# Weight splitting by whole chunks: one ScalarE and one VectorE instruction for two units

## The chip, the cores and the metric

The kernel runs on one core of a Trainium2 chip. The metric is the device time of one execution in microseconds, the median of several runs; lower is better. An execution is also profiled once, and all times of single instructions come from that execution. In this text TensorE is also called PE, ScalarE ACT, VectorE DVE, and GpSimd POOL, as in the rows of the profile.

## The reference

Two layers of a decoder trunk over 256 tokens of width 2048, all in float32. Per layer:

```
h      = rms_norm(x)
proj   = h @ w_in[l]                  # q, k, v, indexer q/k/weights, GLU input, memory q, 3 gates
y_attn = sparse_attention(...) @ w_attn_o[l]      # 64 keys of 256, chosen by an indexer
y_mem  = cross_attention(mq, memory keys/values) @ w_mem_o[l]
y_conv = conformer_conv(glu_in) @ w_conv_o[l] + conv_o_b[l]     # depthwise, 31 taps
x      = x + (g0 * y_attn + g1 * y_mem + g2 * y_conv) @ w_out[l]
x      = x + square(relu(rms_norm(x) @ w_up[l])) @ w_down[l]    # 2048 -> 8192 -> 2048
```

## The kernel before

**Split matmuls.** Each float32 product is made of three reduced-precision ones. A weight `raw` is split into `hi` (raw rounded to the matmul's fp32r type, by ScalarE) and `lo` (raw minus hi, by VectorE); activations have been split in the same way. A product is then a_hi x hi + a_hi x lo + a_lo x hi.

**Chunks and units.** Weights stream from HBM in chunks of 1 MB, 2048 columns per partition. `raw` holds four chunks. A chunk is two units of 1024 columns; `hi` and `lo` hold four units each, that is two chunks. The whole program is 1008 units, used in order. In nearly all of them the unit is 12 matmuls of 512 columns (in the up projection 16 matmuls). In the group G_IKW the weight is only 80 columns wide, so its units are short: 160 columns to split and six small matmuls. Groups G_IQ0 and G_IKW alternate chunk by chunk, steps 16 to 31 of a layer.

**Steps.** Every engine's program is written out as one list of steps, one per unit. In step n ScalarE and VectorE first call `split` for unit n and then do whatever else is planned for that step (`side(n, l)`, `merge`, `mlp`, `x_side`); TensorE does unit n and then the transposes and small matmuls that are planned after it. Within an engine the order is fixed; between engines there are only semaphores. Four of them carry the weights:

- `landed[c]`: the chunk has come from HBM; ScalarE waits for it in the even unit.
- `unit_done`: starts at 4 and goes up by one when TensorE has finished a unit. ScalarE waits in `split` until `unit_done` is n+1, which is to say until unit n-4 is done and its place in `hi` and `lo` is free.
- `hi_ready`: ScalarE to VectorE, one per unit.
- `lo_ready`: VectorE to TensorE, one per unit; the loader on the sync queue waits for two of them before it overwrites a chunk of `raw`.

**What else hangs on the steps.** TensorE waits for results that ScalarE or VectorE produce in a later-numbered step than the unit that it is at. The places that matter here:

- Transposes go through two PSUM banks (`tp`, helper `fill`). A fill waits until the bank's last tile but one has been taken. Most tiles are taken four steps after their fill (`EMPTY_AFTER`).
- `norm_fill` after units 10, 18 and 26 of the output projection (`X_BLOCK_DONE` 12, 20, 28) waits for `scaled`, which VectorE gives in steps 12, 20 and 28, after `add_block` and `scale_block`. The last quarter of the first layer's MLP has the same three places 32 steps later.
- In the output projection unit 6 waits for the second `merged` tile, which VectorE takes in step 8, and the first `merged` fill, after unit 3, waits for `attention_merge` in step 4.
- In each merge block of 32 units, unit 26 needs the accumulator that VectorE empties in step 27 (`GATE_TAKEN`), unit 28 the one it empties in step 29.
- In the first MLP quarter the norm fills after unit 1 wait for `scale_block` in step 2, and unit 3 waits for their taking in step 4. In every quarter unit 4g waits for the accumulator that VectorE frees in step 4g+1.
- The eight index score pairs come after units 49 to 52 and 54 to 57 (`INDEX_PAIR_AT`); a pair waits until ScalarE's relu of the pair before it has emptied the bank, four steps later than that pair's unit.
- The twelve attention heads (`HEAD_AT`, units 77 to 115) send tiles `p` and `o` through the same two banks, mixed with `q`, `conv_out` and `conv_row`.

```
            def side(n, l):
                for _, what, i, j in [f for f in FILLS[l] if taken_at(f, l) == n]:
```

Of the kernel before, what the change touches and what calls it, by code (L numbers as in the profile page):

```python
# [24 lines left out]
F32 = mybir.dt.float32  # L25
F32R = mybir.dt.float32r
I32 = mybir.dt.int32
ALU = mybir.AluOpType
ACT = mybir.ActivationFunctionType
# [111 lines left out]
FILLS = [front_fills(l) for l in range(LAYERS)]  # L141
EMPTY_AFTER = 4
WARM, WARM_ON = 18, 6


def taken_at(f, l):
# [80 lines left out]
def build(nc, x, mem, positions, norm1_g, w_in, q_norm_g, k_norm_g, mem_norm_g, w_mem_kv, mq_norm_g,  # L227
# [3 lines left out]
    with ctx:  # L231
# [4 lines left out]
        def at(name, shape, offset, dt=F32):  # L236
            n = 4
            for s in shape[1:]:
                n *= s
            assert base + offset + n <= nc.sbuf_usable_end, name  # L240
            return nc.alloc_sbuf_tensor_at(name, shape, dt, offset=base + int(offset))


        raw = at("raw", [P, CHUNKS, 4, COL], 0)
        hi = at("hi", [P, 4, 2, COL], 32 * kb, F32R)
        lo = at("lo", [P, 4, 2, COL], 48 * kb, F32R)
# [121 lines left out]
        def sem(name):  # L368
            return ctx.enter_context(nc.semaphore(name))

        landed = [sem(f"landed{c}") for c in range(CHUNKS)]
        hi_ready = sem("hi_ready")
        lo_ready = sem("lo_ready")
        unit_done = sem("unit_done")
# [12 lines left out]
        first_rest = sem("first_rest")  # L387
# [477 lines left out]
        def _(act):  # L865
            here = Place(NAMES)
# [5 lines left out]
            def split(u, w):  # L872
                c = u // 2
                if u % 2 == 0:
                    if u == 0:
                        here.next("group")
                    act.wait_ge(landed[c], here.now("group") * 16)

                if u == 1 and here.now("unit") == 1:
                    act.wait_ge(first_rest, 16)  # L880
                act.wait_ge(unit_done, here.next("unit"))
                act.activation(hi[:, u % 4, :, 0:w], raw[:, c, 2 * (u % 2):2 * (u % 2) + 2, 0:w],  # L882
                               ACT.Copy).then_inc(hi_ready, 1)

            def take(name, out_ap, n=4, w=P, scale=1.0):

# [202 lines left out]
            def merge(first, c, l):  # L1089
                for m in range(4 * UNITS):  # L1090
                    split(m % UNITS, COL)
                    if first:
                        side(FRONT * UNITS + m, l)
                    else:
                        merged_take(m - 11, bass.ds((c - 1) * 4, 4))
                    if m in GATE_TANH:
                        i = GATE_TANH.index(m)
                        act.wait_ge(gate_in, here.next("gate_in"))
                        act.activation(gates[:, i], gates[:, i], ACT.Tanh, scale=0.5).then_inc(gate_tanh, 1)
# [6 lines left out]
            def mlp(first, last):  # L1106
                for m in range(8 * UNITS):
                    split(m % UNITS, COL)
                    if first and m == X_SQUARES:
                        x_squares(CB - 1)  # L1110
                    if first and m == UP_NORM_FILL + 3:
                        for t in range(T):
                            take_norm(CB - 1, t)
                        here.next("rstd_ready")
                    g, r = divmod(m - 8, 4)
                    if r == 0 and g in range(UP_GROUPS):
                        block_done(4 * g + 3)
                        if g >= 2:
                            act.wait_ge(up_square, here.now("up_square") - 1)
                        act.activation(up_half[:, g % 2], acc[:, (1, 0)[g % 2], :, SEQ:2 * SEQ], ACT.Copy  # L1120
                                       ).then_inc(up_half_here, 1)
                    g, r = divmod(m - 10, 4)
                    if r == 0 and g in range(UP_GROUPS):
                        act.wait_ge(up_square, here.next("up_square"))
                        act.activation(bT_hi[:, 2 * g:2 * g + 2], up_sum[:, g % 2], ACT.Copy).then_inc(hid_hi, 1)
                    if last:
                        x_side(m - CB * UNITS)
# [5 lines left out]
            for l in range(LAYERS):  # L1133
                origin[0] = here.now("unit")
                for n in range(FRONT * UNITS):
                    split(n % UNITS, width_of(FRONT_UNITS[n][0]))
                    side(n, l)
                merge(True, 0, l)
                for c in range(1, CB):
                    merge(False, c, l)  # L1140
                for m in range(CB * UNITS):
                    split(m % UNITS, COL)
                    merged_take(m - 7, slice(KT - 4, KT))
                    x_side(m)
                here.next("score", MEM_HEADS + HEADS)
                for qu in range(FFN // D):
                    origin[0] = here.now("unit")
                    mlp(qu == 0, qu == FFN // D - 1 and l < LAYERS - 1)
                here.layer_done()
# [5 lines left out]
        def _(dve):  # L1155
            here = Place(NAMES)
# [16 lines left out]
                dve.sem_inc(waited, 1)  # L1173

            def split(u, w):
                dve.wait_ge(hi_ready, here.next("unit"))
                dve.tensor_tensor(lo[:, u % 4, :, 0:w], raw[:, u // 2, 2 * (u % 2):2 * (u % 2) + 2, 0:w],  # L1177
                                  hi[:, u % 4, :, 0:w].bitcast(F32), ALU.subtract).then_inc(lo_ready, 1)

            def take_low(name, dst, src, n=4, scale=None):  # L1180

# [220 lines left out]
            def merge(first, c, l):  # L1402
                for m in range(4 * UNITS):
                    split(m % UNITS, COL)
                    if first:
                        side(FRONT * UNITS + m, l)
# [46 lines left out]
            def mlp(first, last, l):  # L1453
                for m in range(8 * UNITS):
                    split(m % UNITS, COL)
                    if first and m == 2:
                        add_block(CB - 1, 0, -1)
# [66 lines left out]
            for l in range(LAYERS):  # L1524
                layer_fill[0] = here.now("fill")
                origin[0] = here.now("unit")
                for n in range(FRONT * UNITS):
                    split(n % UNITS, width_of(FRONT_UNITS[n][0]))
                    if l == 0 and n == FIRST_TURNS:
                        turn_tables()  # L1530
                    if n == 3 and l > 0:
                        add_block(CB - 1, 0, -1, squared_rstd)
                        scale_block(CB - 1)
                    side(n, l)
                    if l == 0 and n in (0, 2, 4):
                        first_scale(n // 2 + 1)
# [232 lines left out]
```

## Time and profile before

| | before |
|---|---|
| median of 3 runs | 2873.53 us (2872.09 to 2874.12) |
| profiled execution | 2873.13 us, of which the span of its instructions is 2871.3 us |
| TensorE matmul busy | 2857.5 us |
| VectorE busy | 1747.5 us, of which splitting 1235.3 us in 1008 instructions |
| ScalarE busy | 1426.9 us, of which splitting 1056.0 us in 1008 instructions |
| HBM | 194 GB/s over the span |

A row of the timeline view gives start, duration, engine, line and tiles of an instruction; what stands in brackets at its end is how long the engine had been idle and what ended that. A row of the view by groups gives the count after the x, then busy time in microseconds and the mean of one in nanoseconds.

### The profile page before, as it was taken

To read this page: it belongs to the slowest core of one execution; us is meant where nothing else is said; L and a number is where in the kernel's file an instruction comes from. 1 tells how busy PE (TensorE), PEld (TensorE's weight loads), DVE (VectorE), ACT (ScalarE), POOL (GpSimd) and SP (SyncE) were. 2 spreads that over 40 slices of the span, in tenths; PEclk is the share of its full clock that TensorE was granted. 3 is DMA by queue.
4 is the path that set the end of the run, shared out by engine and by line. 5 is a ranking of instruction groups with operands and counts; after the bars stand their busy time and mean duration, and the time that the engine had idled before them with its cause. 6 is when DMAs were issued, how large, how long until landed. Compare 5 with 4: busy or idle time off the path is not lost.

```text
span 2871.3 us, 34318 instructions
## 1 busy us (share of the span) xinstructions
PE 2857.5 (100%) x13872; PEld 2390.9 (83%) x13872; DVE 1747.5 (61%) x1850; ACT 1426.9 (50%) x1871; POOL 182.6 (6%) x205
## 2 busy tenths in 40 slices
PE   8999999999999999999999999999999999999999
PEld 7878888888888888888888888888888888888887
DVE  6688655555655555556556976556556556455554
ACT  5777644444443434444448775444444444344443
POOL 1125100000000000000001250000000000000000
PEclk9999999999999999999999999999999999999999
DMA  8655566755756556565566455667556565565654
GB/s 297 209 167 175 162 202 206 237 191 193 214 191 191 189 192 187 191 190 184 187 222 212 157 174 172 198 205 235 197 195 188 191 189 185 195 184 192 190 188 147
DMA packets 340319, 557.86 MB, mean 194 GB/s; under 512 B 13216, under 2 KB 144288, under 8 KB 337984
## 3 DMA queue, kind: packets, MB, share of 16 engines
q1 hardware_dynamic: 334416, 526.68, 56.2%
q0 software_dynamic: 5744, 28.97, 3.5%
q8 instruction: 110, 1.80, 0.3%
q14 instruction: 49, 0.40, 0.0%
HBM read 549.32 MB, written 6.29 MB: 194 GB/s over the span
## 4 chain that ended last, share of the span: by engine, by line
PE 98%; DMA 1%; ACT 0%; DVE 0%; issue 0%; SPq 0%; DVEq 0%
PE acc L586 23%; PE acc L588 23%; PE acc L587 23%; PE acc L602 17%; PE acc L603 8%; PE tp L615 2%; DMA raw<-in_w_in 1%; PE sc L676 0%; PE sc L665 0%; PE tp L691 0%; PE sc L662 0%; PE tp L688 0%; ACT hi L882 0%; DMA x_tok<-in_x 0%; PE sc L652 0%
## 5 line engine op out<-in xcount | busy, mean ns | idle before, releaser
L1177 DVE TENSOR_TENSOR lo<-raw,hi 128x1024 fp32r<-128x1024 f32 x1008 | 1235.3, 1227 | 1074.2 <-ACT hi L882 1064.4
L882 ACT ACTIVATE hi<-raw 128x1024 fp32r<-128x1024 f32 x1008 | 1056.0, 1049 | 1382.5 <-PE acc L588 976.3
L602 PE MATMUL acc<-hT,hi 128*128 128x512 f32 x2048 | 724.2, 399 | 0.0
L603 PE MATMUL acc<-hT,lo 128*128 128x256 f32 x2048 | 575.2, 281 | 0.0
L586 PE MATMUL acc<-hi,bT_hi 128*128 128x512 f32 x1408 | 552.3, 392 | 0.0
L588 PE MATMUL acc<-hi,bT_lo 128*128 128x512 f32 x1408 | 548.5, 390 | 0.0
L587 PE MATMUL acc<-lo,bT_hi 128*128 128x512 f32 x1408 | 548.0, 389 | 0.0
L586 PE MATMUL acc<-hi,hT 128*128 128x512 f32 x1280 | 510.0, 398 | 5.0 <-DVE lo L1177 5.0
L588 PE MATMUL acc<-hi,hT 128*128 128x512 f32 x1280 | 499.8, 390 | 0.0
L587 PE MATMUL acc<-lo,hT 128*128 128x512 f32 x1280 | 498.7, 390 | 0.0
L602 PEld LDWEIGHTS acc<-hT,hi 128*128 128x128 f32 x2048 | 384.8, 188 | 95.8
L603 PEld LDWEIGHTS acc<-hT,lo 128*128 128x128 f32 x2048 | 386.9, 189 | 0.3
L588 PEld LDWEIGHTS acc<-hi,bT_lo 128*128 128x128 f32 x1408 | 264.3, 188 | 55.8
L586 PEld LDWEIGHTS acc<-hi,bT_hi 128*128 128x128 f32 x1408 | 264.3, 188 | 55.6 <-DVE bT_lo L1187 0.6
L587 PEld LDWEIGHTS acc<-lo,bT_hi 128*128 128x128 f32 x1408 | 264.4, 188 | 53.4
L586 PEld LDWEIGHTS acc<-hi,hT 128*128 128x128 f32 x1280 | 240.5, 188 | 54.5 <-issue 3.4
L588 PEld LDWEIGHTS acc<-hi,hT 128*128 128x128 f32 x1280 | 240.2, 188 | 51.7
L587 PEld LDWEIGHTS acc<-lo,hT 128*128 128x128 f32 x1280 | 240.7, 188 | 47.2
L927 ACT ACTIVATE tap_part<-uT,tapT 128x256 f32<-128x256 f32 x240 | 101.8, 496 | 2.0 <-ACT relu L1021 1.5
L1227 DVE TENSOR_TENSOR conv_acc<-conv_acc,tap_part 128x1024 f32<-128x1024 f32 x60 | 82.2, 1371 | 0.3
L1479 DVE SCALAR_TENSOR_TENSOR up_sum<-up_sum 128x512 f32<-128x512 f32 x64 | 44.3, 693 | 10.2 <-DVE up_sum L1477 2.9
L1447 DVE SCALAR_TENSOR_TENSOR x_tok<-acc,squared_rstd,x_tok 128x512 f32<-128x512 f32 x64 | 44.9, 743 | 8.6 <-PE acc L588 8.6
(236 smaller groups left out, 1634.0 us busy)
## 6 DMA issues: line engine op xcount, KB each, us to landing
raw<-in_w_in SPq DMA_DIRECT2D x159, 1024.0 KB, 5.0
raw<-in_w_up SPq DMA_DIRECT2D x128, 1024.0 KB, 5.5
raw<-in_w_down SPq DMA_DIRECT2D x128, 1024.0 KB, 5.1
raw<-in_w_out SPq DMA_DIRECT2D x32, 1024.0 KB, 5.1
raw<-in_w_mem_kv SPq DMA_DIRECT2D x16, 1024.0 KB, 5.1
raw<-in_w_attn_o SPq DMA_DIRECT2D x16, 1024.0 KB, 5.1
raw<-in_w_conv_o SPq DMA_DIRECT2D x8, 1024.0 KB, 5.1
raw<-in_w_mem_o SPq DMA_DIRECT2D x8, 1024.0 KB, 5.1
```

Source lines behind the costliest of these rows:

```text
L586: pe.matmul(o, a1, w1, start=first and dk == 0, stop=False)
L587: pe.matmul(o, a1, w2, start=False, stop=False)
L588: mm = pe.matmul(o, a2, w1, start=False, stop=last and dk == 1)
L602: pe.matmul(acc[:, pair, j, :], w1, hT[:, :, kt, :], start=first, stop=last, skip_group_check=True)
L603: mm = pe.matmul(acc[:, pair, j, 0:SEQ], w2, hT_hi[:, kt], start=False, stop=last, skip_group_check=True)
L615: mm = pe.transpose(tp[0:m, b, i, 0:k], tile, ident[0:k, 0:k])
L882: act.activation(hi[:, u % 4, :, 0:w], raw[:, c, 2 * (u % 2):2 * (u % 2) + 2, 0:w], ACT.Copy).then_inc(hi_ready, 1)
L927: ins = act.activation(tap_part[:, k % 2, c], u, ACT.Copy, scale=w)
L1177: dve.tensor_tensor(lo[:, u % 4, :, 0:w], raw[:, u // 2, 2 * (u % 2):2 * (u % 2) + 2, 0:w], hi[:, u % 4, :, 0:w].bitcast(F32), ALU.subtrac ...
L1227: dve.tensor_tensor(conv_acc[:, :, :], conv_acc[:, :, :], tap_part[:, k % 2], ALU.add).then_inc(conv_added, 1)
L1447: ins = dve.scalar_tensor_tensor(xb[:, t], acc[:, pair, t], scaled_by[:, t:t + 1], xb[:, t], ALU.mult, ALU.add)
L1479: dve.scalar_tensor_tensor(up_sum[:, g % 2], up_sum[:, g % 2], 0.0, up_sum[:, g % 2], ALU.max, ALU.mult).then_inc(up_square, 1)
```

## The change

The first 16 units of the program are split as before. From unit 16 on `split` does something only in even steps. ScalarE then waits until unit n-3 is done (`unit_done` at n+2), and writes `hi` of both units of the chunk with one instruction of 2048 columns; VectorE waits for it and writes `lo` of both with one instruction. The semaphores go up by two. All other work stays in its step and behind the split of its step.

```diff
+SPLIT_SINGLY = 16
@@ ScalarE
-                if u == 1 and here.now("unit") == 1:
-                    act.wait_ge(first_rest, 16)
-                act.wait_ge(unit_done, here.next("unit"))
-                act.activation(hi[:, u % 4, :, 0:w], raw[:, c, 2 * (u % 2):2 * (u % 2) + 2, 0:w],
-                               ACT.Copy).then_inc(hi_ready, 1)
+                if here.now("unit") < SPLIT_SINGLY:
...
+                elif u % 2 == 0:
+                    act.wait_ge(unit_done, here.next("unit", 2))
+                    act.activation(hi[:, u % 4:u % 4 + 2, :, 0:w].rearrange("p a k n -> p (a k) n"),
+                                   raw[:, c, :, 0:w], ACT.Copy).then_inc(hi_ready, 2)
@@ VectorE
-                dve.wait_ge(hi_ready, here.next("unit"))
-                dve.tensor_tensor(lo[:, u % 4, :, 0:w], raw[:, u // 2, 2 * (u % 2):2 * (u % 2) + 2, 0:w],
-                                  hi[:, u % 4, :, 0:w].bitcast(F32), ALU.subtract).then_inc(lo_ready, 1)
+                if here.now("unit") < SPLIT_SINGLY:
...
+                elif u % 2 == 0:
+                    dve.wait_ge(hi_ready, here.next("unit", 2))
+                    dve.tensor_tensor(lo[:, u % 4:u % 4 + 2, :, 0:w].rearrange("p a k n -> p (a k) n"),
+                                      raw[:, u // 2, :, 0:w],
+                                      hi[:, u % 4:u % 4 + 2, :, 0:w].rearrange("p a k n -> p (a k) n").bitcast(F32),
+                                      ALU.subtract).then_inc(lo_ready, 2)
```

## Rows read from the trace of the kernel before

**Rows 1.** The page: busy time by engine, and the granted TensorE clock.

```profile
PE 2857.5 (100%) x13872; PEld 2390.9 (83%) x13872; DVE 1747.5 (61%) x1850; ACT 1426.9 (50%) x1871; POOL 182.6 (6%) x205
...
PEclk9999999999999999999999999999999999999999
```

**Rows 2.** Who waited for whom: total us, times, longest us.

```profile
DVE lo L1177 <- ACT hi L882: 1064.4, 823, 3.2
ACT hi L882 <- PE acc L588: 976.3, 627, 3.1
...
PE acc L586 <- DVE lo L1177: 5.0, 4, 2.4
```

**Rows 3.** Groups by line and shape: the two splits, and neighbours in size.

```profile
L1177 DVE TENSOR_TENSOR lo<-raw,hi 128x1024 fp32r<-128x1024 f32 x992 | 1230.6, 1242 | 1069.9 <-ACT hi L882 1060.3
L882 ACT ACTIVATE hi<-raw 128x1024 fp32r<-128x1024 f32 x992 | 1051.1, 1060 | 1376.1 <-PE acc L588 969.9 <-PE acc L603 388.1 <-DMA raw<-in_w_in 12.1
...
L1293 DVE TENSOR_TENSOR wide<-wide,gain 128x2048 f32<-128x2048 f32 x4 | 9.1, 2285 | 0.0
...
L882 ACT ACTIVATE hi<-raw 128x160 fp32r<-128x160 f32 x16 | 5.0, 330 | 6.4 <-PE acc L588 6.3
...
L1177 DVE TENSOR_TENSOR lo<-raw,hi 128x160 fp32r<-128x160 f32 x16 | 4.9, 321 | 4.3 <-ACT hi L882 4.1
```

**Rows 4.** Timeline at unit 6 of the first output projection, all engines.

```profile
654.92 0.68 DVE L1187 SCALAR_TENSOR_TENSOR bT_lo<-tp,bT_hi 128x512 fp32r<-128x512 f32 x1
...
655.41 0.39 PE L588 MATMUL acc<-hi,bT_lo 128*128 128x512 f32 x1
...
655.84 1.06 ACT L882 ACTIVATE hi<-raw 128x1024 fp32r<-128x1024 f32 x1 [1.60 <-PE acc L588]
...
658.79 1.06 ACT L882 ACTIVATE hi<-raw 128x1024 fp32r<-128x1024 f32 x1 [1.89 <-PE acc L588]
```

**Rows 5.** Timeline around unit 10 of the same projection, two engines.

```profile
665.32 1.23 DVE L1177 TENSOR_TENSOR lo<-raw,hi 128x1024 fp32r<-128x1024 f32 x1 [1.55 <-ACT hi L882]
666.47 1.22 DVE L1444 TENSOR_TENSOR x_tok<-acc,x_tok 128x1024 f32<-128x1024 f32 x1
667.83 1.23 DVE L1206 TENSOR_TENSOR xg<-x_tok,gain 128x1024 f32<-128x1024 f32 x1
...
669.19 0.39 PE L588 MATMUL acc<-hi,bT_lo 128*128 128x512 f32 x1
669.42 0.60 PE L615 MATMUL tp<-ident,xg 128*128 128x128 f32 x4
```

**Rows 6.** TensorE's timeline at steps 21 to 24 of the second layer.

```profile
1501.32 0.39 PE L588 MATMUL acc<-hi,hT 128*128 128x512 f32 x1
...
1502.57 0.28 PE L652 MATMUL sc<-hT,hi 128*80 128x256 f32 x1
...
1503.70 0.28 PE L652 MATMUL sc<-hT,hi 128*80 128x256 f32 x1
```

**Rows 7.** Groups by line and shape: what else is on the waits' path.

```profile
L1447 DVE SCALAR_TENSOR_TENSOR x_tok<-acc,squared_rstd,x_tok 128x512 f32<-128x512 f32 x64 | 44.9, 743 | 8.6 <-PE acc L588 8.6
...
L1477 DVE TENSOR_TENSOR up_sum<-acc,up_half 128x512 f32<-128x512 f32 x64 | 43.7, 683 | 0.0
...
L1418 DVE SCALAR_TENSOR_TENSOR gates<-acc,rstd,gate_bias 128x512 f32<-128x512 f32 x48 | 33.7, 743 | 6.5 <-DMA conv_bias<-in_conv_o_b 6.5
...
L1021 ACT ACTIVATE relu<-sc 128x768 f32<-128x768 f32 x16 | 12.8, 797 | 0.0
```

**Rows 8.** Busy time by stretch: us, then each engine's, granted clock, DMA share, GB/s.

```profile
730.00:800.00 70.00, 70.00 (x401) 60.87 (x400) 42.45 (x46) 33.45 (x41) 4.97 (x9) 1.00 0.72 216
...
100.00:250.00 150.00, 150.00 (x707) 121.70 (x706) 126.30 (x170) 118.17 (x203) 39.47 (x35) 1.00 0.55 180
```

**Rows 9.** ScalarE's timeline in the first layer's heads.

```profile
285.17 1.06 ACT L882 ACTIVATE hi<-raw 128x1024 fp32r<-128x1024 f32 x1
286.13 0.58 ACT L889 ACTIVATE y_tok<-tp 128x512 f32<-128x512 f32 x1
```

More of the change, by code:

```diff
@@ L877, in split @@
                     act.wait_ge(landed[c], here.now("group") * 16)
-                if u == 1 and here.now("unit") == 1:
-                    act.wait_ge(first_rest, 16)
-                act.wait_ge(unit_done, here.next("unit"))
-                act.activation(hi[:, u % 4, :, 0:w], raw[:, c, 2 * (u % 2):2 * (u % 2) + 2, 0:w],
-                               ACT.Copy).then_inc(hi_ready, 1)
+                if here.now("unit") < SPLIT_SINGLY:
+                    if u == 1 and here.now("unit") == 1:
+                        act.wait_ge(first_rest, 16)
+                    act.wait_ge(unit_done, here.next("unit"))
+                    act.activation(hi[:, u % 4, :, 0:w], raw[:, c, 2 * (u % 2):2 * (u % 2) + 2, 0:w],
+                                   ACT.Copy).then_inc(hi_ready, 1)
+                elif u % 2 == 0:
+                    act.wait_ge(unit_done, here.next("unit", 2))
+                    act.activation(hi[:, u % 4:u % 4 + 2, :, 0:w].rearrange("p a k n -> p (a k) n"),
+                                   raw[:, c, :, 0:w], ACT.Copy).then_inc(hi_ready, 2)
             def take(name, out_ap, n=4, w=P, scale=1.0):
@@ L1175, in split @@
             def split(u, w):
-                dve.wait_ge(hi_ready, here.next("unit"))
-                dve.tensor_tensor(lo[:, u % 4, :, 0:w], raw[:, u // 2, 2 * (u % 2):2 * (u % 2) + 2, 0:w],
-                                  hi[:, u % 4, :, 0:w].bitcast(F32), ALU.subtract).then_inc(lo_ready, 1)
+                if here.now("unit") < SPLIT_SINGLY:
+                    dve.wait_ge(hi_ready, here.next("unit"))
+                    dve.tensor_tensor(lo[:, u % 4, :, 0:w], raw[:, u // 2, 2 * (u % 2):2 * (u % 2) + 2, 0:w],
+                                      hi[:, u % 4, :, 0:w].bitcast(F32), ALU.subtract).then_inc(lo_ready, 1)
+                elif u % 2 == 0:
[4 more added lines that the diff above has]
+                                      ALU.subtract).then_inc(lo_ready, 2)
             def take_low(name, dst, src, n=4, scale=None):
```

## The prediction

> **What bounds the kernel now.** I read the page first: matmuls are busy for 2857.5 us of a span of 2871.3, at the full clock in all 40 slices [rows 1]. VectorE and ScalarE are 61% and 50% busy. So work taken off them is worth nothing by itself, and the change can act only through what TensorE waits for. The view of waits says the same: ScalarE waits for TensorE before 627 of its splits, VectorE waits for ScalarE before 823, and TensorE waits for a split 4 times, 5.0 us in all [rows 2]. The whole pipeline follows TensorE with a lead. The timeline tells how large that lead is and which steps have less of it.
>
> **The cost of the instructions.** VectorE's pair: the trace has the same operation with 2048 columns in float32, 2.285 us [rows 3]. ScalarE's pair has no row. From 160 to 1024 columns it goes from 330 to 1060 ns, 0.845 ns a column; another 1024 columns make 1.93 us [rows 3]. The bounds are 1.83 (if columns beyond 1024 cost 0.75 ns) and 2.12 (twice 1.06, nothing saved). In place of 2.48 + 2.12 us a chunk takes 2.29 + 1.93, so each of the two engines loses at most some 95 us of busy time over 488 full chunks (8 more are narrow). Value: nothing, since neither is the bound; the cover is TensorE's own 2.72 us per unit, and without that cover it would be these sums.
>
> The Trainium skill (VectorE: DVE Perf Modes, the section on the TRN2 errata) says that ops reading SBUF pay a fixed cost per instruction, which a larger tile pays once, and gives ScalarE 224 cycles plus one per column at 1.2 GHz. By that the pair would take 1.89 us by estimate and the sum below would be about 2 us lower; the VectorE row agrees with the rule's direction.
>
> **When things are ready.** Call E(k) the end of unit k. The last matmuls of units 5 and 10 start at 655.41 and 669.19 [rows 4, 5], five units in 13.78 us; less the 0.17 of a wait, explained below, a unit takes 2.72.
> Before: step n starts on ScalarE up to 0.08 after E(n-4), `hi` takes 1.06, VectorE follows 0.02 later with 1.23. `lo` is there at E(n-4) + 2.4, three units minus 2.4, so 5.75 us ahead of its use. Other work of step n starts on VectorE at E(n-4) + 2.3 (the next instruction starts 0.08 before the end of the one before it: 665.32 + 1.23, then 666.47 [rows 5]).
> After, step n even: ScalarE starts at E(n-3) + 0.06 and has `hi` 1.93 later; VectorE's `lo` comes at E(n-3) + 4.32, other work starts at E(n-3) + 4.22. Weights are then 2 x 2.72 - 4.32 = 1.1 us ahead of their use: enough for the plain stretches. But VectorE's other work of an even step comes one unit plus 1.9 us later than before, 4.6 us in all; that of an odd step 1.9 us later.
>
> How early must a result be? In rows 4 VectorE's take ends at 655.60, the last matmul of unit 5 ends at 655.80 (655.41 + 0.39), and still unit 6 ended late: ScalarE, which starts behind each unit's end, started at 655.84 and then 658.79, 2.95 apart, of which 0.06 is the scatter of its starts, so unit 6 took 2.89 instead of 2.72. So a result must come 0.37 before E of the unit ahead of it, or the difference is a stall.
>
> **The places, one by one.** The stall is (start of the step's other work) + (its duration) + 0.37 - (time until E of the unit before the wait).
>
> 1. `norm_fill` after unit 10 waits for step 12, an even one. L1444 and L1206 take 2.59 from the first's start to the second's end [rows 5]. Before, they ended at 669.06 and the fill started at 669.42, right behind unit 10. After: 4.22 + 2.59 + 0.37 - 2.72 = 4.46. Three places in two output projections: 26.8. In the last quarter of layer 0's MLP the add is two L1447, 1.41 with overlap [rows 7]; 4.65 x 3 = 14.0.
> 2. Unit 6 of the output projection waits for step 8. Unit 8's split itself now waits for E(5), so nothing of it is covered: 4.22 + 0.68 + 0.37 = 5.27, twice: 10.5. Fill after unit 3 waits for step 4: 4.22 + 2.59 + 0.37 - 5.44 = 1.74, twice: 3.5.
> 3. Unit 26 of a merge block, step 27 (odd, so counted from E(23), two units ahead): 4.22 + 1.41 (two L1418 [rows 7]) + 0.07 + 0.37 - 5.44 = 0.63, in the six later blocks: 3.8. Unit 28 would be 0.3 late but that stall covers it.
> 4. First MLP quarter: fill after unit 1 waits for step 2, 1.5; then unit 3 for step 4, 0.6 more. Twice: 4.4. Unit 4g and step 4g+1: 4.22 + 0.68 + 0.08 + 0.37 = 5.35 against two up units (401 matmuls touch 70 us of them, 16 to a unit, so 2.8 each [rows 8]), 5.6: no stall, by 0.25 us. There are 64 such places.
> 5. The short units. Two G_IKW units last 1.84 us together when one has a fill (last matmuls at 1501.32, 1502.57, 1503.70, 1.14 and 1.13 from end to end, with a fill of 0.43 in each [rows 6], so 0.70 without); units 20, 28 and 32 follow such a pair and their chunk is begun only at its start: 4.32 + 0.37 - 1.8 = 2.85, three times 8.6. The fill after unit 22 waits for a bank that VectorE empties in step 24: 4.22 + 0.68 + 0.37 - 1.14 = 4.13. Two layers: 25.4.
> 6. Index pairs after units 51, 55 and 57 wait for a relu in an even step that begins only when that unit is done: 0.06 + 1.93 - 0.09 + 0.80 [rows 7] + 0.07 + 0.37 = 3.14, three times 9.4; those after 50 and 54 about 1.2 and 0.4, since ScalarE has key rows to take in step 52. Two layers: 22.0.
> 7. The heads. The fill after unit 109 waits for a bank emptied in step 112, as in 2: 5.3. The last fill after unit 93 waits already (it needs the take at 286.13, behind the exps and the split at 285.17 [rows 9]); now 0.87 of a longer split and about 1.2 of exps come in between: 2.1. Fills after 88, 90, 96, 98 and 108 by the same sum 1.5, 0.5, 0.6, 1.2 and 1.3; units 114 and 116 0.2. Two layers: 25.4. This is the roughest of the terms, as the waits follow each other closely.
> 8. Unit 16 of layer 0 (VectorE is held up there by the memory rows) 1.0; unit 6 of layer 1 0.6; dense steps near 70 of each layer 0.5 twice. 2.6.
>
> Sum: 26.8 + 14.0 + 10.5 + 3.5 + 3.8 + 4.4 + 25.4 + 22.0 + 25.4 + 2.6 = 138.4 us in some 60 stalls. Each is taken once with the unit ends of before, which is fair because every later wait is counted from the stalled units. 2871.3 + 138.4 = 3009.7; the profiled execution lasted 1.8 us more than its span, and the median of runs is 0.4 above that: 3012 us. Bounds of ScalarE's pair (1.83 to 2.12) move it by 6 down and 11 up. Transfers play no part: a chunk is asked for later by 2 us but lands well before its split, since only 12.1 us of ScalarE's waits were for DMA [rows 3].
>
> The Trainium skill (Perfetto Trace Analysis, Optimizing Scalar/DVE Operations) speaks against this change: grouping helps where an engine is saturated, and where ScalarE or VectorE are not saturated but cause bubbles elsewhere, smaller instructions let work be done sooner. The sum above is that rule at work; by its other half (grouping pays) the time would stay at 2873, since the saving is on engines with slack.
>
> **The rivals.**
> - *The lead absorbs it* (not slower). The weights stay 1.1 us ahead; if the results of even steps are not really waited for at TensorE where the program says so, nothing is left: 2873. For it: TensorE waits for almost nothing now [rows 2]. Against: in rows 4 a wait of just this kind shows, 0.17 us with the old lead. It decides only if the stalls add up to less than 5.7 us, 4% of my sum. Chance 0.03.
> - *The stalls overlap.* A stall gives all engines time, so neighbours in 5, 6 and 7 may cover one another. If those three groups keep half of their 72.8, the time is 2976; case of 2930 to 2985. Chance 0.2.
> - *The clock falls.* The granted clock is full in every slice [rows 1], and the longest waits for a split were 2.4 us [rows 2]. After the change 15 stalls are longer than 4 us (nine in 1, two in 2, two in 5, two in 7). If in each the clock falls from 2.4 to 1.2 GHz for the length of one unit, that is 2.72 us each, 41 us: 3053. Case of 3035 to 3095. Nothing in the trace shows a fall; nothing in it has so long a stall either. Chance 0.2. The Trainium skill (TensorE: Matmul & The Clock Gate) describes such a gate, which halves the clock after TensorE has been idle; no row here shows it.
> - *VectorE or ScalarE backs up.* Between 100 and 250 us VectorE is busy 126.3 of 150 us and ScalarE 118.2 [rows 8]. With a lead of 1.1 us instead of 5.75, bursts of work show. Counted above as far as I could; it would add 10 to 20 us, within the range.
>
> **The numbers.** My forecast, stalls as summed (2985 to 3035): 0.57; overlap 0.2; clock 0.2; absorbed 0.03. Range 2940 to 3062 leaves out the absorbed case and the upper part of the clock case. A change within 0.2% (5.7 us) is what a measurement of this kernel can't tell from none. Slower 0.97, same 0.02, faster 0.01.
>
> **What the next profile would show.** L882 with 128x2048 x488 at 1.93 us and L1177 at 2.29; ScalarE and VectorE each busy less by at most 95 us. In the waits, TensorE's L615 behind DVE xg (nine times, about 4.5 us), L586 behind DVE lo (2.9 us, units 20, 28, 32), sc L676 behind ACT relu (3.1 us), L586 behind DVE bT_lo (5.3 us, twice). In the up projection no waits, unit pitch unchanged at 2.8. I would be wrong if L1293 and the line through 1.06 are bad guides to the pairs, if the up projection's 64 places with 0.25 us to spare begin to stall, or if PEclk shows anything but 9.

## The result, and the profile after

The changed kernel takes 3079.2 us (3075.2 to 3083.3), before 2872.8: ratio 1.0716, 95% interval 1.0703 to 1.0728. The forecast was 3012, with a range up to 3062. The sign was right, and so were the places except for two stalls in each merge block; the time lies 17 us above the range.

The page of the changed kernel, busy time by engine and the granted clock of TensorE in 40 slices, answers to [rows 1]:

```profile
span 3073.0 us, 33806 instructions
PE 2923.3 (95%) x13872; PEld 2424.1 (79%) x13872; DVE 1669.7 (54%) x1354; ACT 1329.9 (43%) x1375; POOL 187.9 (6%) x205
...
PEclk9999999999999999999998999999999999999999
```

ScalarE and VectorE did lose work, 97 and 78 us of busy time, and it bought nothing. TensorE was busy for 99.5% of the span and is now for 95%. The splits, by groups, answer to [rows 3] (the means include eight narrow chunks):

```profile
L1188 DVE TENSOR_TENSOR lo<-raw,hi 128x2048 fp32r<-128x2048 f32 x496 | 1137.1, 2293 | 1347.6 <-ACT hi L888 1345.6
L888 ACT ACTIVATE hi<-raw 128x2048 fp32r<-128x2048 f32 x496 | 938.9, 1893 | 1572.6 <-PE acc L589 1136.2
```

What TensorE waits for now, from the view of waits (total us, times, longest; "ACTq" is ScalarE's sequencer giving a bank free), beside [rows 2]:

```profile
ACT gates L1105 <- DVE gates L1431: 54.1, 16, 3.9
...
PE tp L616 <- DVE xg L1219: 42.5, 12, 4.5
...
PE acc L587 <- DVE lo L1188: 28.0, 27, 2.8
...
PE sc L677 <- ACTq L1030: 19.3, 10, 3.0
...
PE tp L616 <- DVE cT_lo L1200: 10.2, 2, 5.1
PE acc L587 <- DVE bT_lo L1200: 10.2, 2, 5.1
```

These rows can be laid beside the terms of the prediction: the norm fills 40.8 forecast for nine places, 42.5 measured with the first MLP's two and the start in it; unit 6 of the output projections 10.5 against 10.2, the fill after unit 109 10.6 against 10.2; the index pairs 22 against 19.3. The first row is not a wait of TensorE; no term of the forecast had it. Before the change it was small:

```profile
ACT gates L1099 <- DVE gates L1418: 6.3, 2, 3.2
```

The timeline at unit 6 of the first output projection, ScalarE, VectorE and TensorE, is the same place as [rows 4]:

```profile
715.55 1.91 ACT L888 ACTIVATE hi<-raw 128x2048 fp32r<-128x2048 f32 x1 [5.37 <-PE acc L589]
...
717.56 2.29 DVE L1188 TENSOR_TENSOR lo<-raw,hi 128x2048 fp32r<-128x2048 f32 x1 [5.28 <-ACT hi L888]
719.77 0.68 DVE L1200 SCALAR_TENSOR_TENSOR bT_lo<-tp,bT_hi 128x512 fp32r<-128x512 f32 x1
...
720.51 0.79 PE L587 MATMUL acc<-hi,bT_hi 128*128 128x512 f32 x1 [5.08 <-DVE bT_lo L1200]
721.10 0.63 PE L588 MATMUL acc<-lo,bT_hi 128*128 128x512 f32 x1
721.53 0.63 PE L589 MATMUL acc<-hi,bT_lo 128*128 128x512 f32 x1
```

The pair begins on ScalarE when unit 5 has ended, VectorE's take starts 4.22 us later (the prediction's terms give 4.16 from there), and TensorE has stood still for 5.08. Then the matmuls run, but 0.43 us apart and 0.63 long. Before the change they were 0.39 long and started 0.23 apart at this place, at the full clock:

```profile
654.96 0.39 PE L586 MATMUL acc<-hi,bT_hi 128*128 128x512 f32 x1
655.19 0.39 PE L587 MATMUL acc<-lo,bT_hi 128*128 128x512 f32 x1
```

The busy time of stretches around the stall after the change (engines in order PE, PEld, DVE, ACT, POOL, then the granted clock) tells why:

```profile
715.00:719.00 4.00, 0.43 (x2) 0.01 (x1) 1.44 (x1) 2.40 (x2) 0.00 (x0) 1.00 0.93 341
719.30:726.00 6.70, 5.49 (x13) 4.33 (x14) 1.15 (x2) 0.00 (x0) 0.00 (x0) 0.50 0.47 169
730.00:739.00 9.00, 7.04 (x32) 5.49 (x30) 4.83 (x3) 2.84 (x2) 0.00 (x0) 1.00 0.33 117
739.80:746.60 6.80, 5.28 (x15) 4.33 (x16) 1.31 (x2) 1.45 (x4) 0.00 (x0) 0.50 0.46 157
```

At 719.3, still in the stall, the granted clock falls from 2.4 to 1.2 GHz (0.50), and it stays there until 726; behind the next stall it does so again. The mean granted clock of the whole span tells what that is worth, before and after:

```profile
core 0: 2871.3 us, clock 1.000
```

```profile
core 0: 3073.0 us, clock 0.980
```

(1 - 0.980) x 3073 = 61 us, an upper figure, as part of the low stretches lies in the stalls themselves. The span grew by 201.7 us. So up to 61 us are the clock, which the forecast left out, and at least 140 are stalls. A nearer split comes from the low stretches themselves: all of them in this trace are 125 us long, and TensorE is busy in 105 of these. At the full clock that work would have taken about half, so the clock's part is some 53 us, and the stalls are some 149 against 138.4 forecast (an estimate from this one trace; 1.7 us of the 53 belong to a low stretch at the very start, which again_1 below has too, without a stall of the change).

### The profile page after: what moved, and what is told of

It reads as the page before. It is cut to its first block, busy times and chain, and to the rows that moved or that the text cites. A ratio compares the mean times of both kernels' runs of the same rounds, so it can differ in the third digit from the quotient of the medians.

```text
span 3073.0 us, 33806 instructions
## 1 busy us (share of the span) xinstructions
PE 2923.3 (95%) x13872; PEld 2424.1 (79%) x13872; DVE 1669.7 (54%) x1354; ACT 1329.9 (43%) x1375; POOL 187.9 (6%) x205
## 4 chain that ended last, share of the span: by engine, by line
PE 82%; DVE 7%; ACT 6%; issue 3%; DMA 1%; ACTq 0%; DVEq 0%; SPq 0%
PE acc L587 19%; PE acc L589 19%; PE acc L588 19%; PE acc L603 15%; PE acc L604 8%; ACT hi L888 5%; DVE lo L1188 4%; PE tp L616 2%; DVE gates L1431 1%; DMA raw<-in_w_in 1%; DVE conv_acc L1240 1%; DVE xg L1219 0%; PE sc L677 0%; PE tp L692 0%; DVE x_tok L1457 0%
## 5 line engine op out<-in xcount | busy, mean ns | idle before, releaser
L1188 DVE TENSOR_TENSOR lo<-raw,hi 128x2048 fp32r<-128x2048 f32 x496 | 1137.1, 2293 | 1347.6 <-ACT hi L888 1345.6
L888 ACT ACTIVATE hi<-raw 128x2048 fp32r<-128x2048 f32 x496 | 938.9, 1893 | 1572.6 <-PE acc L589 1136.2
L587 PE MATMUL acc<-hi,bT_hi 128*128 128x512 f32 x1408 | 563.3, 400 | 10.2 <-DVE bT_lo L1200 10.2
L588 PE MATMUL acc<-lo,bT_hi 128*128 128x512 f32 x1408 | 556.7, 395 | 0.0
L589 PE MATMUL acc<-hi,bT_lo 128*128 128x512 f32 x1408 | 556.3, 395 | 0.0
L587 PE MATMUL acc<-hi,hT 128*128 128x512 f32 x1280 | 519.8, 406 | 31.8 <-DVE lo L1188 28.0
L589 PE MATMUL acc<-hi,hT 128*128 128x512 f32 x1280 | 506.5, 396 | 0.0
L588 PE MATMUL acc<-lo,hT 128*128 128x512 f32 x1280 | 505.5, 395 | 0.0
L587 PEld LDWEIGHTS acc<-hi,hT 128*128 128x128 f32 x1280 | 244.4, 191 | 91.9 <-DVE lo L1188 26.6
L589 PEld LDWEIGHTS acc<-hi,hT 128*128 128x128 f32 x1280 | 244.2, 191 | 53.6
L616 PE MATMUL tp<-ident,xg 128*128 128x128 f32 x128 | 23.3, 322 | 42.5 <-DVE xg L1219 42.5
L616 PEld LDWEIGHTS tp<-ident,xg 128*128 128x128 f32 x128 | 17.7, 165 | 49.3 <-DVE xg L1219 47.2
```

The source lines that it names most:

```text
L587: pe.matmul(o, a1, w1, start=first and dk == 0, stop=False)
L588: pe.matmul(o, a1, w2, start=False, stop=False)
L589: mm = pe.matmul(o, a2, w1, start=False, stop=last and dk == 1)
L616: mm = pe.transpose(tp[0:m, b, i, 0:k], tile, ident[0:k, 0:k])
L888: act.activation(hi[:, u % 4:u % 4 + 2, :, 0:w].rearrange("p a k n -> p (a k) n"), raw[:, c, :, 0:w], ACT.Copy).then_inc(hi_ready, 2)
L1188: dve.tensor_tensor(lo[:, u % 4:u % 4 + 2, :, 0:w].rearrange("p a k n -> p (a k) n"), raw[:, u // 2, :, 0:w], hi[:, u % 4:u % 4 + 2, :, 0: ...
```

## The experiments

The column "rest", the stalls, is the growth of the profiled span over 2871.3 us less the clock's part, which is (1 - mean granted clock) x span; with a clock given to 0.001 that part is good to 1.5 us. TensorE is idle in part of the low stretches, so the clock's part is an upper figure and the rest a lower one. For the stalls of one place the text uses growth: how much longer a unit took, from the end of the unit before to its own, than the same unit before the change.

| kernel | median us | ratio to before (95%) | mean clock | clock's part | rest |
|---|---|---|---|---|---|
| the change | 3079.2 | 1.0716 (1.0703 to 1.0728) | 0.980 | 61 | 140 |
| order_only | 3012.9 | 1.0482 (1.0467 to 1.0498) | 0.983 | 51 | 89 |
| pair_in_odd_step | 2941.7 | 1.0235 (1.0220 to 1.0250) | 0.995 | 15 | 53 |
| keep_busy | 3053.9 | 1.0622 (1.0607 to 1.0638) | 0.991 | 27 | 147 |
| pairs_mlp | 2874.4 | 1.0000 (0.9991 to 1.0010) | 1.000 | 0 | 2 |
| act_pair_only | 3016.7 | 1.0497 (1.0481 to 1.0512) | 0.988 | 36 | 105 |
| dve_pair_only | 3015.7 | 1.0494 (1.0478 to 1.0509) | 0.984 | 48 | 96 |
| front_singly | 3036.5 | 1.0565 (1.0550 to 1.0581) | 0.983 | 52 | 115 |
| again_1 | 2883.8 | 1.0032 (1.0020 to 1.0045) | 0.999 | 3 | 8 |
| again_2 | 2898.0 | 1.0086 (1.0071 to 1.0101) | 0.997 | 9 | 15 |
| again_3 | 2919.1 | 1.0156 (1.0139 to 1.0173) | 0.993 | 20 | 26 |
| tanh_later | 3074.5 | 1.0693 (1.0679 to 1.0708) | 0.977 | 71 | 130 |

**order_only: the wait and the order, without the large instructions.**

```diff
                 elif u % 2 == 0:
                     act.wait_ge(unit_done, here.next("unit", 2))
-                    act.activation(hi[:, u % 4:u % 4 + 2, :, 0:w]...
+                    for v in range(2):
+                        act.activation(hi[:, u % 4 + v, :, 0:w], raw[:, c, 2 * v:2 * v + 2, 0:w],
+                                       ACT.Copy).then_inc(hi_ready, 1)
```

and VectorE in the same way, waiting for each half.

> Edit: the pair's wait (unit n-3 done) and its place (both splits in the even step, ahead of that step's other work) are kept, but each engine uses two instructions of 1024 columns again. Theory (late other work): the loss comes from the wait and the order, not from the size of the instructions; VectorE's other work then starts 3.4 us after E(n-3) instead of 4.2, so some 50 stalls behind VectorE are 0.8 us shorter and a few falls of the clock go with them: 3020 to 3040 us. Rival (the size): two small instructions are as before, 2873 to 2880.

3012.9 us, so 139 of the 206 us come without any large instruction; the rival, that the size alone costs, is out. The size adds the rest: with pairs VectorE can't start on the first half while ScalarE is at the second. The stalls at units 20, 28 and 32 shrink by some 2 us each, and the later merge blocks take no longer than before the change. The index pairs' stalls did not shrink (ScalarE is as late as with the pair); those behind VectorE did, by one microsecond each at the norm fills, where the longest went from 4.5 to 3.6:

```profile
PE tp L616 <- DVE xg L1220: 32.3, 12, 3.6
...
PE sc L677 <- ACTq L1031: 20.0, 10, 3.1
```

**pair_in_odd_step: the large instructions, behind the even step's other work.**

```diff
-                elif u % 2 == 0:
+                elif u % 2 == 1:
                     act.wait_ge(unit_done, here.next("unit", 2))
-                    act.activation(hi[:, u % 4:u % 4 + 2, :, 0:w]...
+                    act.activation(hi[:, u % 4 - 1:u % 4 + 1, :, 0:w]...
```

and VectorE in the same way.

> Edit: the pair instructions stay, but are issued in the odd step, so the even step's other work goes ahead of them. Theory: stalls that wait for an even step vanish (norm fills, unit 6 of the output projection, units 14 and 22 of the merge blocks, the index pairs after 51, 55 and 57, the fill after 109); left are units 20, 28 and 32 of each layer (17 us), the odd steps (gate 27, heads, about 14) and some 10 us of clock: 2905 to 2925 us. Rival (weights' lead): the weights come no earlier than in the changed kernel, so if their lead of 1.1 us is what costs, it stays at 3079.

2941.7 us: two thirds of the loss gone with every pair still in place, so the lead of the weights is not what costs, except at the short units, where TensorE still waits for them. It is above what I expected by 17 us or more, though. The norm fills and unit 6 no longer wait, and the fill after unit 109 waits 1.3 us instead of 5.1:

```profile
ACT gates L1105 <- DVE gates L1431: 29.2, 10, 3.8
...
PE tp L616 <- DVE cT_lo L1200: 2.6, 2, 1.3
...
PE tp L616 <- DVE xg L1219: 0.4, 1, 0.4
```

What is left, by the ends of the same units in both traces: steps 0 to 47 hold 16.0 and 14.4 us (units 20, 24, 28 and 32, and the clock behind some of them), the heads 9.5 and 10.3, the later merge blocks 5.3 per layer, of which 0.7 at unit 26 and 1.1 at unit 28 in each block. Some of this is new: unit 24 waits for its weights, 2.5 us in each layer, and the fill after unit 108 stalls for 3.3 us instead of 1.1. The heads and the merge blocks of both layers hold 30.5 us where the expectation had about 14, and that is most of the miss.

**keep_busy: the changed kernel, with TensorE kept at work in eleven of its stalls.**

```diff
                 if t == 0:
+                    if here.now("unit") % 504 >= 216 and b < CB - 1:
+                        for i in range(36):
+                            pe.transpose(sc[:, 0, 0, 0:P], ident[:, :], ident[:, :])
                     pe.wait_ge(scaled, here.next("scaled"))
@@
                     if m == 6:
+                        for i in range(42):
+                            pe.transpose(sc[:, 0, 0, 0:P], ident[:, :], ident[:, :])
                         emptied(("merged", 1))
```

> Edit: the changed kernel, and TensorE runs 36 dummy transposes of 128 columns before each of the nine waiting norm fills and 42 before unit 6 of each output projection; they fit into the stalls there. Theory (the clock's fall is a cost of its own behind long stalls): about 26 us come back, 3053 us, the granted clock stays at 1.00 in those stretches, and each of those stalls shrinks to its own 4.5 or 5.3 us. Rival (the stalls were simply longer than worked out): no gain, 3079, or a loss of some us.

3053.9 us, 25 less, as worked out. The same stretch of the first output projection, in the change and here:

```profile
677.00:800.00 123.00, 103.13 (x432) 83.11 (x431) 59.21 (x38) 39.91 (x33) 0.57 (x1) 0.92 0.47 157
```

```profile
677.00:795.00 118.00, 114.51 (x589) 95.90 (x589) 60.33 (x38) 40.19 (x34) 0.57 (x1) 1.00 0.51 169
```

The clock stays full, and the output projections now last 20.4 us longer than before the change, both of them, and the last MLP quarter of layer 0 14.0. The prediction's terms for these are (26.8 + 10.5 + 3.5) / 2 = 20.4 and 14.0. In the changed kernel it was 29.2, 29.4 and 20.7. This settles both halves of the matter for these eleven places: the stalls were sized rightly, and the rest behind them is the clock.

**pairs_mlp: pairs only where no stall was worked out.** A pair is used in units 256 to 503 of a layer, without the last 32 of layer 0.

```diff
+def split_singly(n):
+    m = n % 504
+    return m < 256 or 472 <= n < 504
```

> Edit: pairs only in units 256 to 503 of each layer (the MLP without its first 8 units), and not in the last 32 of layer 0; everything else is split singly. These stretches have no place where I worked out a stall, but hold the 64 up-projection waits with 0.25 us to spare. Theory: 2873 us, plus or minus 2. Rival (size of the instruction, or a lead of 1.1 us, costs everywhere): 232 of the 496 pairs, so 50 to 95 us slower, 2925 to 2970.

2874.4 us, ratio 1.0000: no difference that can be measured, with 232 pairs, and TensorE waits for nothing in them. ScalarE's pair took 1.92 us, where the line through 160 and 1024 columns gave 1.93, and VectorE's 2.29:

```profile
L1194 DVE TENSOR_TENSOR lo<-raw,hi 128x2048 fp32r<-128x2048 f32 x232 | 532.0, 2293 | 598.4 <-ACT hi L894 598.4
...
L894 ACT ACTIVATE hi<-raw 128x2048 fp32r<-128x2048 f32 x232 | 444.8, 1917 | 784.3 <-PE acc L610 407.1 <-PE acc L595 377.2
```

The up projection's waits with 0.25 us to spare held. This version matches the kernel before and does not beat it; none of the runs does, as TensorE is busy 99.5% of the span there.

**act_pair_only and dve_pair_only: one part of the change each.** The other engine keeps its code of before.

> Edit: ScalarE's pair as in the change, VectorE splits singly in each step as before. Theory: VectorE's other work of even steps starts 1.05 us earlier than with both pairs (3.17 instead of 4.22 us after E(n-3)), and the first unit of a chunk is split 1.05 us earlier, so some 25 stalls are that much shorter and the index pairs' stalls stay: 3030 to 3050 us. Rival (VectorE's large instruction is what costs): back to 2873 to 2890.

> Edit: VectorE's pair as in the change, ScalarE splits singly as before. Theory: ScalarE's own results (index relus, takes) are in time again, 22 us less, and VectorE's other work of even steps starts 0.87 us earlier, 3.35 us after E(n-3), some 30 us less, plus 20 to 30 us of clock: 2985 to 3015 us. Rival (ScalarE's large instruction is what costs): back to 2873 to 2890.

3016.7 and 3015.7 us. Neither large instruction alone takes the blame, and neither rival holds. dve_pair_only came out at the edge of the expectation, with the index pairs no longer waiting (0.01 and 0.03 us of growth in units 48 to 64 against 13.0 and 13.1 in the change). It has stalls that the change has not: the heads grow by 22.9 and 22.2 us instead of 15.9 and 16.2. In the view of waits TensorE stands still there behind these results of VectorE:

```profile
PE tp L616 <- DVE moT_lo L1193: 6.9, 2, 3.5
PE tp L616 <- DVE oT_lo L1193: 6.0, 2, 3.0
```

A likely reason, not tested by itself, is that VectorE's pair now waits for ScalarE's second single split, which stands behind ScalarE's other work. act_pair_only is 13 us under the expectation: the stalls at units 14 and 22 of the merge blocks, which I had not seen, are gone there too (growth of the later merge blocks 2.1 us per layer instead of 7.5).

**front_singly: steps 0 to 47 of each layer split as before.** Its edit is `return n % 504 < 48` in the same function.

> Edit: the changed kernel with steps 0 to 47 of each layer split singly. Theory: exactly what the trace shows there goes, 18.2 us in layer 0 and 21.9 in layer 1, stalls and clock together: 3037 to 3043 us. Rival (lateness that is avoided there shows up in later steps instead): over 3055 us.

3036.5 us, half a microsecond under the expectation. These stalls do not move on to later steps; they are a cost of their own.

**again_1, again_2, again_3: stalls of chosen length in the kernel before.**

```diff
                             dve.wait_ge(gain_in, here.next("gain_in", 16))
+                        for again in range(2):
+                            block = x_tok[:, :, b * COL:(b + 1) * COL]
+                            link(dve.tensor_tensor(xg[:, b % 2], block,
+                                                   over(gain[:, b * COL:(b + 1) * COL], 1, T), ALU.mult))
                         scale_block(b)
```

> Edit: the kernel before, and VectorE does the multiply of scale_block once more in each of the nine steps that a norm fill waits for, so that TensorE stalls there; nothing else is changed. One more is 1.38 us, of which 0.18 was to spare: nine stalls of 1.2 to 1.4 us, 11.4 in all, 2885.5 us. Both theories of the clock expect no fall here.

> Edit: as again_1 with two repetitions: nine stalls of 2.6 to 2.8 us, 23.8 in all, 2898 us by the stalls alone. If the clock falls only behind stalls of over 4 us, as my prediction had it, that is the time. If stalls of some 3 us are enough, as behind units 20 and 28 in the changed kernel, some of the nine places show a granted clock of 0.5 behind them and the time is 2902 to 2912 us.

> Edit: as again_1 with three repetitions: nine stalls of 4.0 to 4.2 us, 36.2 in all, 2910 us by the stalls alone. Prediction's rule (a fall costs one unit, 2.7 us, behind stalls of over 4 us): 2910 to 2920. What the changed kernel shows (about 2.3 us of clock for each long stall, the low stretches being 3.4 or 6.8 us long): 2928 to 2938 us.

2883.8, 2898.0 and 2919.1 us. One repetition costs 1.25 us, not 1.38. Place by place (growth of the unit behind the fill): with one repetition nine times 1.02 to 1.21; with two, five times 2.28 to 2.46 and four times 3.85 to 4.04; with three, once 3.55 and eight times 4.85 to 6.42. The higher values are those where the granted clock fell. In again_2 that is this place, the stretch with the stall and the one behind it:

```profile
718.00:722.00 4.00, 1.94 (x12) 1.36 (x10) 3.93 (x4) 0.48 (x1) 0.00 (x0) 1.00 0.13 46
722.40:725.80 3.40, 3.40 (x10) 2.62 (x9) 2.04 (x3) 2.02 (x4) 0.00 (x0) 0.50 0.53 130
726.00:734.00 8.00, 8.00 (x39) 6.63 (x38) 3.48 (x4) 3.67 (x4) 0.00 (x0) 1.00 0.65 199
```

So a stall of 2.1 to 2.3 us of idle TensorE brought a fall in four of nine places, of 3.3 to 3.5 in eight of nine, of 0.8 to 1.0 in none (again_1's low stretches are one at the very start and one at the very end); a fall cost 1.3 to 2.9 us. The totals alone would have misled: again_2's is the 2898 that was given for stalls without any fall, and again_3's lies in the range of the prediction's rule, 2910 to 2920. Both are luck, since each repetition was shorter than reckoned and falls made up for it. The traces decide: all these stalls are under 4 us, and the clock fell behind twelve of them. The prediction's limit of 4 us is out; its price of 2.7 is at the upper end.

**tanh_later: the term that the sum left out.**

```diff
-GATE_TAKEN, GATE_TANH = [12, 20, 27], [13, 21, 28]
+GATE_TAKEN, GATE_TANH = [12, 20, 27], [14, 22, 28]
```

> Edit: the changed kernel with the gates' tanh of steps 13 and 21 moved on ScalarE by one step, to 14 and 22, behind the next chunk's split. Theory (a wait that my sum left out): ScalarE's tanh in an odd step now waits for VectorE's gate work of the even step before it, which comes 4.6 us later than it did, and so holds up the next chunk's split; the stalls of 1.15 us before unit 14 and 0.5 us before unit 22 of each later merge block vanish, 10 us in six blocks, 3069 us. Rival (those stalls come from VectorE's own backlog behind the gate work): they stay, 3079.

The median is 3074.5 us, 4.7 less and not 10, and by the total alone this would not be decided. The traces decide it. In the change ScalarE's tanh waits for VectorE's gate work of the step before, the next split starts behind it, and TensorE stands still for the weights (a later merge block, unit 14):

```profile
457.85 1.40 DVE L1431 SCALAR_TENSOR_TENSOR gates<-acc,rstd,gate_bias 128x512 f32<-128x512 f32 x2
459.28 1.06 ACT L1105 ACTIVATE gates<-gates 128x1024 f32<-128x1024 f32 x1 [3.87 <-DVE gates L1431]
460.25 1.90 ACT L888 ACTIVATE hi<-raw 128x2048 fp32r<-128x2048 f32 x1
462.25 2.29 DVE L1188 TENSOR_TENSOR lo<-raw,hi 128x2048 fp32r<-128x2048 f32 x1 [3.00 <-ACT hi L888]
464.60 0.50 PE L587 MATMUL acc<-hi,hT 128*128 128x512 f32 x1 [0.82 <-DVE lo L1188]
```

In tanh_later no wait of ScalarE's gates for VectorE is left among the waits (16 times, 54.1 us in the change), and the later merge blocks last 2.4 and 2.5 us longer than before the change instead of 7.5 in each layer, so the 10 us are there. What they won was lost elsewhere. The first merge block lies among the heads, so the edit touches these too: a fill that waits for `oT_lo` stands still for 2.0 us in each layer, where it was 1.1 in the change:

```profile
PE tp L616 <- DVE oT_lo L1198: 3.9, 2, 2.0
```

The clock falls behind it in both layers; the heads grow by 19.1 us each instead of 15.9 and 16.2. The rest is the clock at places that the edit does not touch: the index pairs wait as long as in the change and grow by 18.9 and 18.6 us instead of 13.0 and 13.1. The mean clock is 0.977 instead of 0.980. Why one execution has more of the falls than another was not settled.

## Why the prediction was wrong

- **What bounds the kernel:** right. Less work on ScalarE and VectorE was worth nothing (pairs_mlp, ratio 1.0000).
- **The cost of the pairs:** right. 1.92 and 2.29 against 1.93 and 2.29. The Trainium skill's figure (VectorE: DVE Perf Modes, the section on the TRN2 errata), 1.89 by estimate, is 0.03 under the measured one.
- **When things are ready:** right to 0.1 us. The take at unit 6 starts 4.22 us behind the pair's start, where the terms give 4.16.
- **Places 1, 2, 5, 6:** right within a few microseconds, as the waits and keep_busy show. Place 4's up projection did not stall. The heads (7), called the roughest, were 15.9 and 16.2 us per layer, some 1.5 to 2 of it clock, 12.7 forecast. Place 8's dense steps near 70 were 1.9 us per layer instead of 0.5.
- **Place 3 was short of a wait.** It said "Unit 26 of a merge block [...] 0.63". ScalarE's tanh in steps 13 and 21 waits for VectorE's gate work, which now comes so late that the next chunk's split is held up: 1.15 us at unit 14, 0.5 at unit 22, 10 us in all. I had counted what TensorE waits for, and what is late on VectorE, but not ScalarE waiting for VectorE ahead of a split.
- **The sum** of 138.4 stands against some 149: it is short by about the 10 us of this wait, and the smaller misses nearly cancel. That alone would have left the time within the range.
- **The step that failed is the clock.** "*The clock falls.* [...] If in each the clock falls from 2.4 to 1.2 GHz for the length of one unit, that is 2.72 us each, 41 us: 3053. [...] Chance 0.2." It was worked out as a rival, whose case of 3035 to 3095 holds the measured time, and the forecast put it at nothing. Its mechanism is shown by keep_busy. Some 53 us were lost to it, not 41, because it took only the 15 stalls of over 4 us, where stalls of 2 to 3 us bring falls too (again_2). In the profiled execution of the change the clock fell behind 24 of the 27 stalls of 2.5 us of idle TensorE and more, most of those at units 20, 28, 32 and the index pairs among them, and behind none of the others, of which the longest were 1.6. The argument "nothing in it has so long a stall either" was right and cut both ways: the trace of before holds no row on what a stall does to the clock, so the range had to allow for a fall behind the shorter of the long stalls as well.
- The rival that stalls overlap was wrong (front_singly: no shift), as was the absorbed case. The Trainium skill's rule against the change (Perfetto Trace Analysis, Optimizing Scalar/DVE Operations), to break instructions up where engines that are not saturated cause bubbles on others, agrees with the runs: order_only, with smaller instructions and nothing else, is 66 us faster than the change.

## What to carry to other kernels

Where an in-order engine does a large job and small ones in turn, work out when the small ones start, not only when the large one ends: making the job wait for one unit more and moving it ahead cost 139 us without growing any instruction, and letting the even step's small work go first gave back two thirds of the loss. Batch where the trace shows nothing hanging on the steps; there it was free. And where a change puts a matmul engine that never stood still into stalls of 2 us and more, add to each a microsecond or two for its clock (here some 53 us for 27 such stalls), as a part of the forecast and not as a rival.

## What the runs showed of the hardware that was not expected

- The granted clock fell behind stalls as short as 2.0 to 2.3 us of idle TensorE (again_2, four of nine; tanh_later, the two behind `oT_lo`), and behind none of again_1's nine of 0.8 to 1.0.
- The low stretch can begin in the stall, before TensorE resumes (719.3 and 720.5), and lasts while matmuls already run back to back. The Trainium skill (TensorE: Matmul & The Clock Gate, HAM oscillation) tells of this pattern, waits that make the next burst start cold; these traces agree. In keep_busy dummy transposes in the wait avoided it, and the change took 25 us less.
- With the same program the loss to the clock differs between executions: the change ran 3075 to 3083 us with mean clocks of 0.980 to 0.977, the longer executions at the lower clock, where the kernel before stayed within 2.4 us.
